# Input weights by column chunk, convolution and pool ahead of attention, residual reloads on GpSimd's DMA queue and V spills on ScalarE's

## The chip, the cores and the metric

The kernel runs on the 8 cores of one Trainium2 chip. Each core takes one prompt of 2048 tokens and 4 of the 32 decode sequences (8 tokens each), so nothing is exchanged between cores. The metric is device time in microseconds (us) of the slowest core, median of several runs.

## The reference

Two layers, each on 2080 tokens (32 sampled ones first, then the prompt) of width 1024:

```
h = rmsnorm(x, norm1_g);  u, q, k, v, gb, gc, gh = split(h @ w_in)      # 1024 x 2560
y_pool = pool_mix(u)                  # causal means over 2, 4, 8, 16 tokens, then 64x64 matrices
q, k   = rope(rmsnorm(q)), rope(rmsnorm(k))
y_attn = 3 groups of 2 heads: banded attention at window/dilation 128/1, 512/4, 2048/16,
         merged by their softmax denominators (sampled tokens attend to a cache)
y_conv = gb * conv3(gc * gh)          # causal, width 3
x = x + concat(y_pool, y_attn, y_conv) @ w_out                          # 768 x 1024
x = x + square(relu(rmsnorm(x, norm2_g) @ w_up)) @ w_down               # 1024 x 4096 x 1024
```

New pool, convolution and key/value states are also written out. Matmuls take bf16; the residual stream stays f32.

## The kernel before

Tokens are split into 5 blocks of 416 (`NB`, `BL`); a matmul has 128 rows of contraction, 128 output channels and 416 tokens. Attention goes in 4 prompt blocks of 512 tokens (`blk`) and one item for the sampled tokens (`None`).

**Who sets the order.** The order of instructions on every engine is made on the host by a planner (`Planner`, L298). Work is written as generators with a priority (the smaller number goes first) that wait for events; at each modelled moment the planner emits the ready operation with the best priority and adds its modelled cost. On the chip every engine then runs its own list strictly in order, and waits on semaphores only for real dependences (`Sched._deps`, L100), so an instruction that waits holds all that stand behind it on its engine. An event that the planner waited for is not itself a wait on the chip.

**A layer.** `norm` (L853) squares a block on ScalarE, sums on TensorE or GpSimd, and writes the normalised block `HT` by eight VectorE instructions (L889). `qkv` (L1039) makes one item of 256 tokens for one group: 16 matmuls (L1071), square, reduce, scale (L1104), GpSimd multiply (L1110), rotation (L1117, L1118), GpSimd cast (L1148), transposes. There are 24 prompt items and 3 sample items per layer, run in the order of `QORDER`. For groups 1 and 2, V goes out to DRAM and back to be reordered (`vshuffle` L1199: spill at L1200, load at L1210, both on SP's DMA queue). `att_pair`, `att_dil` and `att` do scores (L1248, L1289), exponential, and PV (L1273, L1299). `conv_item` (L988) and `pool_item` (L936) project one block with `proj` (L921, L923: 8 matmuls each) and run chains on VectorE, ScalarE and GpSimd; each block waits for the one before it. `out_proj` (L1391) adds to the residual, then `norm` again, then `up` (L1417) and `down` (L1436) in 4 chunks of the 4096 hidden channels.

**Priorities** in layer base: sample items 95, `qkv` 100 + 50 blk, `att` 90 + 50 blk, `pool_item` 120 + 40 b, `conv_item` 121 + 40 b and up.

**Memory.** The five f32 blocks of x occupy slots `SC, SP_, SQ_, SK, SV`. During attention these are scratch: convolution lives in `SC`, pool in `SP_`, qkv in `SQ_`, caches and packed queries in `SK`, V in `SV`. So x is parked in DRAM (`park` L903), and `reload` (L911) brings each block back when its slot's tenants are done, on SP's queue, before `out_proj`. One arena at `AR` holds `WQ` (q, k, v columns), `WA` (the others), the keys, `WO` and two of three `PB`, and later the MLP's `WU[0], WD[0], WU[1], WD[1]`, 16384 bytes each in this order. So the first `w_up` chunk lies over `WQ`, the first `w_down` chunk over `WQ` and `WA`.

**Loads.** `w_in` arrives in row chunks (`load_wq` L811, `load_wa` L824, two rows of 128 each, all columns), and `conv_item` and `pool_item` wait for all four `wa` chunks. The second DMA of each `wa` chunk (L827) waits for the first (L826). At the start x comes on SP's queue (`load_x0` L798; block 1 waits for a weight chunk, block 4 for the first norm; x0 and x4 share an area, x2 and x3 land in `SC` and `SP_`), weights on GpSimd's. `copy_caches` (L1458) copies old cache rows from DRAM to DRAM on SP's queue. GpSimd's queue alone casts f32 weights to bf16 on the way.

Of the kernel before, what the change touches and what calls it, by code (L numbers as in the profile page):

```python
# [24 lines left out]
NB = 5  # L25
# [272 lines left out]
class Planner:  # L298
# [3 lines left out]
    def __init__(self, S):  # L302
        self.S = S
        self.evs = {}
        self.now = 0.0
        self.seq = 0
        self.heap = []
        self.free = {e: 0.0 for e in COMPUTE + ("sp",)}
        self.ready = {e: [] for e in COMPUTE + ("sp",)}
        self.busy = {e: 0.0 for e in COMPUTE + ("sp",)}  # L310
        self.dma_free = 0.0
        self.live = 0
# [75 lines left out]
    def start(self, eng):  # L388
# [23 lines left out]
        if len(op) > 4:  # L412
            self.dma_free = max(self.dma_free, self.now) + op[4] / 230e3
            done = max(self.dma_free, self.now) + 2.0
# [71 lines left out]
def build_program():  # L486
# [103 lines left out]
    QS = M([128, 3, 64], BF16)  # L590
    KTS = M([128, 3, 32], BF16)
    for g in range(3):
        S.region(("qs", g))
        S.region(("kts", g))
# [3 lines left out]
    SS4 = [M([128, 8], F32, ("ss4", i)) for i in range(4)]  # L598
    RS4 = [M([128, 8], F32, ("rs4", i)) for i in range(4)]
    NP = 3  # L600
    PB = [M([128, 1024], BF16, ("pb", 2))]
# [21 lines left out]
    mf = Mem(MIX_OFF, M.off)  # L623
    RL = [mf([128, BL], F32, ("rl", i)) for i in range(2)]
    AT = []
    for i in range(2):
        o = mf.off
        AT.append(mf([128, 8, BL], BF16))
        for f in range(8):
            S.region(("at", i, f), o + f * 2 * BL, o + (f + 1) * 2 * BL)  # L630
    AR = M.off
    M.off += 65536
    ma = Mem(AR)
    o = ma.off
    WQ = ma([128, 8, 1152], BF16)
    for i in range(4):
        S.region(("wq", i), o + i * 4608, o + i * 4608 + 4608)
    o = ma.off
    WA = ma([128, 8, 1408], BF16)
    for i in range(4):  # L640
        S.region(("wa", i), o + i * 5632, o + i * 5632 + 5632)
# [10 lines left out]
    assert ma.off == AR + 49152  # L652
    WO = [ma([128, 2, 1024], BF16, ("wo", i)) for i in range(3)]
    PB = [ma([128, 1024], BF16, ("pb", i)) for i in range(2)] + PB
    assert ma.off == AR + 65536
    ma = Mem(AR)
    WU, WD = [], []
    for i in range(2):
        for nm, lst in (("wu", WU), ("wd", WD)):
            o = ma.off  # L660
            lst.append(ma([128, 8, 1024], BF16))
            for h in range(2):
                S.region((nm, i, h), o + h * 8192, o + h * 8192 + 8192)
# [9 lines left out]
    SLOT0 = ["m", "a", SC, SP_, "m"]  # L673
    XM = view(MIX_OFF, [128, 1, 8, BL], F32)
    XA = view(AR + 49152, [128, 1, 8, BL], F32)
    for c in range(8):
        S.region(("x", "m", c), MIX_OFF + c * BL * 4, MIX_OFF + (c + 1) * BL * 4)
        S.region(("x", "a", c), AR + 49152 + c * BL * 4, AR + 49152 + (c + 1) * BL * 4)
# [4 lines left out]
    SLOTR = [SC, SP_, SQ_, SK, SV]  # L683
# [37 lines left out]
    CVT = [m([128, 13, 128], BF16, ("cvt", 0))]  # L721
    QP = []
# [18 lines left out]
    def pool(n, fn, r, w, two=True):  # L741
        return ("pool", 0.15 + n * (0.0021 if two else 0.0011), lambda: [S.op("pool", fn, r, w)], [(0.0, r, w)])
# [18 lines left out]
    PGC, PCA, PRL, PPS, PCK, PSS, PNORM = Pool(range(2)), Pool(range(2)), Pool(range(2)), Pool(range(2)), Pool([0]), Pool(range(3)), Pool([0])  # L761

    PVST = Pool(range(3))
    evs = K.evs
# [27 lines left out]
    def prologue():  # L792
        yield ops(dve(1, lambda e: e.memset(EPSC, EPS), [], ["epsc"]),
                  pool(128, lambda e: e.memset(ONESR[:, :].bitcast(F32), 1.0), [], ["onesr"], False),
                  pool(128, lambda e: e.memset(ONESB, 1.0), [], ["onesb"], False),
                  pool(192, lambda e: e.memset(QS, 0.0), [], [("qs", g) for g in range(3)], False))

    def load_x0():  # L798
        for b in range(NB):
            Xs, s, si = stage0(b)  # L800
            if b == 1:
                yield wait(ev("wq", 0, 1))
            if b == 4:
                yield wait(ev("ht", 0, 0))
            for h in range(2):
                yield ops(ld(lambda e, h=h: e.dma_start(out=Xs[:, si, 4 * h:4 * h + 4, :], in_=xin[b, :, 4 * h:4 * h + 4, :]), 851968,
                             r=[("wq", 1)] if b == 1 else [], w=[("x", s, c) for c in range(4 * h, 4 * h + 4)], slot=("xl", s, h)))
                for c in range(4 * h, 4 * h + 4):
                    K.fire(ev("xr", 0, b, c))

    def load_wq(l, i):  # L811
        wv = w_in[l].rearrange("(c p) n -> p c n", p=128)
        yield ops(ldc(lambda e: e.dma_start(out=WQ[:, 2 * i:2 * i + 2, :], in_=wv[:, 2 * i:2 * i + 2, 256:1408]), 1179648, w=[("wq", i)], slot=("wq", i)))
# [10 lines left out]
    def load_wa(l, i):  # L824
        wv = w_in[l].rearrange("(c p) n -> p c n", p=128)
        yield ops(ldc(lambda e: e.dma_start(out=WA[:, 2 * i:2 * i + 2, 0:256], in_=wv[:, 2 * i:2 * i + 2, 0:256]), 262144, w=[("wa", i)], slot=("wa", i)),  # L826
                  ldc(lambda e: e.dma_start(out=WA[:, 2 * i:2 * i + 2, 256:1408], in_=wv[:, 2 * i:2 * i + 2, 1408:2560]), 1179648, w=[("wa", i)], slot=("wa", i)))  # L827
        K.fire(ev("wa", l, i))
# [6 lines left out]
    def load_f(l, fb, nm):  # L835
        i = fb % 2
        for h in range(2):
            if nm == "wu":
                src = w_up[l].rearrange("(c p) f -> p c f", p=128)[:, 4 * h:4 * h + 4, fb * 1024:(fb + 1) * 1024]
                dst = WU[i][:, 4 * h:4 * h + 4, :]  # L840
            else:
                src = w_down[l][fb * 1024:(fb + 1) * 1024, :].rearrange("(c p) n -> p c n", p=128)[:, 4 * h:4 * h + 4, :]
                dst = WD[i][:, 4 * h:4 * h + 4, :]
            yield ops(ldc(lambda e: e.dma_start(out=dst, in_=src), 2097152, w=[(nm, i, h)], slot=(nm, i, h)))  # L844
        K.fire(ev(nm, l, fb))
# [7 lines left out]
    def norm(l, which, b, X, s, si, src, out_ev, before=(), on_pe=False):  # L853
# [35 lines left out]
        yield ops(*[dve(BL + 100, lambda e, c=c: e.scalar_tensor_tensor(out=HT[:, c, BL * b:BL * b + BL], in0=X[:, si, c, :], scalar=NG[:, l, which, c:c + 1], in1=rst, op0=ALU.mult, op1=ALU.mult),  # L889
# [21 lines left out]
    def reload(l, b, after):  # L911
# [3 lines left out]
        for h in range(2):  # L915
            yield ops(ld(lambda e: e.dma_start(out=X[:, s, 4 * h:4 * h + 4, :], in_=src[b, :, 4 * h:4 * h + 4, :]), 851968,
                         r=([("park", b)] if l else []), w=[("x", s, c) for c in range(4 * h, 4 * h + 4)], slot=("xl", s, h)))
            for c in range(4 * h, 4 * h + 4):
                K.fire(ev("xres", l, b, c))

    def proj(l, col0, b):  # L921
        bi = yield acq(BANKS)
        yield ops(pe([(BL, lambda e, d=d: e.matmul(bank(bi)[:, 0:BL], lhsT=WA[:, d, col0:col0 + 128], rhs=HT[:, d, BL * b:BL * b + BL], start=(d == 0), stop=(d == 7)),  # L923
                       [("wa", d // 2), ("ht", b, d)], [("ps", bi)]) for d in range(8)]))
# [5 lines left out]
    def mix_free(l, b):  # L930
        if l == 0:
            return [ev("ht", 0, 0), ev("ht", 0, 4)]
        o = ORDER[l - 1][3]
        return [ev("up", l - 1, 3, x, fc) for x in o for fc in range(8)] + [ev("down", l - 1, 3, x) for x in (o[:-1] if b < 2 else o)]

    def pool_item(l, b, pc):  # L936
        yield wait(ev("ht", l, b), ev("free", l, SP_), ev("pw", l), *[ev("wa", l, i) for i in range(4)])
# [6 lines left out]
        bi = yield from proj(l, 128 * pc, b)  # L944
# [18 lines left out]
        yield ops(*[dve(L, lambda e, ps_=ps_, win=win: e.scalar_tensor_tensor(out=dt[ps_, o:BL], in0=win[ps_, 15:W], scalar=INVW[ps_, pc:pc + 1], in1=Uv[ps_, 15:W], op0=ALU.mult, op1=ALU.subtract),  # L963
# [24 lines left out]
    def conv_item(l, b, cc):  # L988
        yield wait(ev("ht", l, b), ev("free", l, SC), *[ev("wa", l, i) for i in range(4)])
# [6 lines left out]
        bc = yield from proj(l, 256 + 384 + 128 * cc, b)  # L996
# [11 lines left out]
        bh = yield from proj(l, 256 + 768 + 128 * cc, b)  # L1008
# [15 lines left out]
        for k in (1, 2):  # L1024
            o4 = [dve(L, lambda e: e.scalar_tensor_tensor(out=ca[:, o:BL], in0=Zv[:, k:k + L], scalar=cw(k), in1=ca[:, o:BL], op0=ALU.mult, op1=ALU.add), [kz, kc, "convw"], [kc])]
# [5 lines left out]
        bb = yield from proj(l, 256 + 128 * cc, b)  # L1031
# [7 lines left out]
    def qkv(l, blk, g, pr):  # L1039
# [6 lines left out]
        yield wait(ev("gqk", l), ev("vones", l), ev("qpz", l), *[ev("free", l, s) for s in (SQ_, SK, SV)], *[ev("wq", l, i) for i in range(4)], *[ev("ht", l, b) for b in hb])  # L1046
        if l > 0:
            yield wait(*[ev("um", l - 1, 3, b, fc) for b in range(NB) for fc in range(8)])
# [16 lines left out]
        def lhs(d, j):  # L1065
            if smp:
# [3 lines left out]
        wg = WQ.rearrange("p d (k n) -> p d k n", k=3)  # L1070
        yield ops(pe([(384, lambda e, d=d, j=j, jj=jj: e.matmul(pq[0:R, jj, 0:384].rearrange("p (k n) -> p k n", k=3), lhsT=lhs(d, j), rhs=wg[:, d, :, 128 * g:128 * g + 128], start=(d == 0), stop=(d == 7)),  # L1071
                       [("wq", d // 2)] + [("ht", b, d) for b in hb], [kp[jj]]) for jj, j in enumerate(tis) for d in range(8)]))
# [585 lines left out]
```

## Time and profile before

| | us |
|---|---|
| median of 3 runs (1600.55 to 1610.0) | 1606.35 |
| profiled execution, its own time | 1609.34 |
| its span on the slowest core (core 7; the others from 1582.2) | 1607.4 |
| TensorE busy in the span (89%) | 1424.3 |
| VectorE busy (53%) | 857.4 |
| ScalarE busy (30%) | 478.5 |
| GpSimd busy (22%) | 347.4 |
| DMA moved | 133.32 MB, mean 83 GB/s |

The table of stretches says for each part of the span how long each engine was busy, the TensorE clock that was granted (1.00 is the 2.4 GHz level) and the mean busy share of the 16 DMA engines. The chain of waits lists, in order of time, the pieces that ended last. An engine's timeline gives start, duration, line, operation, and in brackets the idle time before and what ended it.

### The profile page before, as it was taken

To read this page: it belongs to the slowest core of one execution; us is meant where nothing else is said; L and a number is where in the kernel's file an instruction comes from. 1 tells how busy PE (TensorE), PEld (TensorE's weight loads), DVE (VectorE), ACT (ScalarE), POOL (GpSimd) and SP (SyncE) were. 2 spreads that over 40 slices of the span, in tenths; PEclk is the share of its full clock that TensorE was granted. 3 is DMA by queue.
4 is the path that set the end of the run, shared out by engine and by line. 5 is a ranking of instruction groups with operands and counts; after the bars stand their busy time and mean duration, and the time that the engine had idled before them with its cause. 6 is when DMAs were issued, how large, how long until landed. Compare 5 with 4: busy or idle time off the path is not lost.

```text
span 1607.4 us, 26919 instructions; the slowest of 8 cores (1582.2 to 1607.4 us)
## 1 busy us (share of the span) xinstructions
PE 1424.3 (89%) x8606; PEld 801.8 (50%) x8606; DVE 857.4 (53%) x1547; ACT 478.5 (30%) x1065; POOL 347.4 (22%) x426
## 2 busy tenths in 40 slices
PE   2778788779999999999977789868699999999998
PEld 1344455434555555555544455534355555555554
DVE  1667667467444444445676666746854444444443
ACT  2544345424112212113433444532412111211211
POOL 2344344344000000012434344323500000000000
PEclk9789889899999999999999999989899999999999
DMA  8758541999223023033264452189920601400112
GB/s 184 167 75 71 111 111 34 137 234 171 49 49 58 1 53 53 1 63 76 86 148 57 68 133 74 36 127 241 169 50 1 105 1 28 79 1 1 44 69 102
DMA packets 67897, 133.32 MB, mean 83 GB/s; under 512 B 25832, under 2 KB 35112, under 8 KB 67376
## 3 DMA queue, kind: packets, MB, share of 16 engines
q0 software_dynamic: 27648, 54.14, 23.2%
q1 hardware_dynamic: 40112, 77.47, 18.1%
q8 instruction: 72, 1.18, 0.3%
q14 instruction: 65, 0.53, 0.2%
HBM read 159.71 MB, written 47.89 MB: 129 GB/s over the span
## 4 chain that ended last, share of the span: by engine, by line
PE 69%; DMA 10%; DVE 8%; issue 5%; POOL 4%; ACT 3%; SPq 1%; DVEq 0%; ACTq 0%; POOLq 0%
PE psum L1441 28%; PE psum L1425 27%; PE psum L923 5%; PE psum L1071 4%; DMA vspill<-big 4%; DMA big<-xin 3%; PE psum L1402 3%; DVE big L889 3%; DMA big<-w_in 2%; POOL sqr L875 1%; POOL big L1110 1%; POOL big L956 1%; DVE big L1118 1%; DVE big L1117 1%; DMA kv_p<-big 1%
## 5 line engine op out<-in xcount | busy, mean ns | idle before, releaser
L1425 PE MATMUL psum<-big 128*128 128x416 bf16 x2560 | 464.3, 341 | 4.3 <-DVE big L1406 2.2
L1441 PE MATMUL psum<-big 128*128 128x416 bf16 x2560 | 461.0, 339 | 1.5 <-DVE big L1431 1.5
L1430 ACT ACTIVATE big<-psum 128x416 f32<-128x416 f32 x320 | 165.1, 517 | 650.8 <-PE psum L1425 426.4
L1425 PEld LDWEIGHTS psum<-big 128*128 128x128 bf16 x2560 | 251.0, 98 | 206.8 <-issue 9.6
L1441 PEld LDWEIGHTS psum<-big 128*128 128x128 bf16 x2560 | 250.0, 98 | 201.5 <-issue 3.0
L1431 DVE TENSOR_TENSOR big<-psum,big 128x416 bf16<-128x416 f32 x320 | 187.9, 591 | 284.5 <-ACT big L1430 274.0
L1444 DVE TENSOR_TENSOR big<-psum,big 128x416 f32<-128x416 f32 x320 | 188.5, 591 | 200.4 <-PE psum L1441 199.7
L923 PE MATMUL psum<-big 128*128 128x416 bf16 x880 | 179.3, 355 | 10.6 <-ACT big L984 5.6
L1071 PE MATMUL psum<-big 128*128 128x384 bf16 (+1 forms) x816 | 156.5, 350 | 10.0 <-ACT big L1260 3.0
L889 DVE SCALAR_TENSOR_TENSOR big<-big 128x416 bf16<-128x416 f32 x160 | 120.7, 823 | 49.7 <-ACT big L886 42.6
L875 POOL TENSOR_TENSOR sqr<-sqr,big 128x416 fp32r<-128x416 f32 x98 | 107.9, 1101 | 172.1 <-ACT big L874 161.9
L923 PEld LDWEIGHTS psum<-big 128*128 128x128 bf16 x880 | 87.3, 102 | 80.5 <-issue 25.3
L1071 PEld LDWEIGHTS psum<-big 128*128 128x128 bf16 (+1 forms) x816 | 82.5, 104 | 73.9 <-issue 31.4
L1402 PE MATMUL psum<-big 128*128 128x416 bf16 x480 | 94.4, 356 | 15.4 <-DVE big L1406 13.2
L1110 POOL TENSOR_TENSOR big<-big 128x512 f32<-128x512 f32 (+1 forms) x54 | 66.7, 1238 | 184.2 <-DVE big L1104 170.2
L844 POOL DMA_DIRECT2D big<-w_up x16 | 12.2, 767 | 334.3 <-PE psum L1425 333.8
L874 ACT ACTIVATE big<-big 128x416 f32<-128x416 f32 x98 | 52.7, 547 | 98.4 <-DVE big L1406 62.5
L1402 PEld LDWEIGHTS psum<-big 128*128 128x128 bf16 x480 | 47.9, 102 | 58.3 <-issue 25.6
L956 POOL TENSOR_TENSOR big<-big 128x430 f32<-128x430 f32 (+7 forms) x72 | 64.7, 903 | 36.3 <-ACT big L952 28.4
L1406 DVE TENSOR_TENSOR big<-psum,big 128x416 f32<-128x416 f32 x80 | 45.3, 587 | 45.5 <-PE psum L1402 25.5
L864 PE MATMUL psum<-sqr,onesr 128*128 128x416 f32 x48 | 24.5, 567 | 40.3 <-ACT sqr L863 37.8
L1117 DVE TENSOR_TENSOR big<-big 128x128 f32<-128x128 f32 (+1 forms) x108 | 42.4, 393 | 27.7 <-POOL big L1110 21.8
(98 smaller groups left out, 892.9 us busy)
## 6 DMA issues: line engine op xcount, KB each, us to landing
big<-xin SPq DMA_DIRECT2D x20, 832.0 KB, 12.1
big<-w_up POOLq DMA_DIRECT2D x16, 1024.0 KB, 15.4
big<-w_down POOLq DMA_DIRECT2D x16, 1024.0 KB, 13.3
kv_s<-c SPq DMA_DIRECT2D x8, 2040.0 KB, 40.2
big<-w_in POOLq DMA_DIRECT2D x16, 576.0 KB, 8.7
xpark<-big SPq DMA_DIRECT2D x10, 832.0 KB, 3.6
big<-xpark SPq DMA_DIRECT2D x10, 832.0 KB, 15.7
yout<-big SPq DMA_DIRECT2D x20, 416.0 KB, 2.4
```

The source lines that it names most:

```text
L875: K.spawn(freeing(pool(BL, lambda e, i=i: e.tensor_tensor(out=acc, in0=acc.bitcast(F32), in1=SS[i], op=ALU.add), [ka, ("ss", i)], [ka]), P ...
L889: yield ops(*[dve(BL + 100, lambda e, c=c: e.scalar_tensor_tensor(out=HT[:, c, BL * b:BL * b + BL], in0=X[:, si, c, :], scalar=NG[:, l, wh ...
L923: yield ops(pe([(BL, lambda e, d=d: e.matmul(bank(bi)[:, 0:BL], lhsT=WA[:, d, col0:col0 + 128], rhs=HT[:, d, BL * b:BL * b + BL], start=(d ...
L956: return pool(n, lambda e: e.tensor_tensor(out=out, in0=a, in1=b_, op=ALU.add), r, w)
L1071: yield ops(pe([(384, lambda e, d=d, j=j, jj=jj: e.matmul(pq[0:R, jj, 0:384].rearrange("p (k n) -> p k n", k=3), lhsT=lhs(d, j), rhs=wg[:, ...
L1110: yield ops(pool(256 * J, lambda e: e.tensor_tensor(out=qf[0:R, 0:J, 0:256], in0=qf[0:R, 0:J, 0:256], in1=GQK[0:R].unsqueeze(1).to_broadca ...
L1402: yield ops(pe([(BL, lambda e, c=c: e.matmul(bank(bi)[:, 0:BL], lhsT=WO[c // 2][:, c % 2, 128 * oc:128 * oc + 128], rhs=mix(c, b), start=( ...
L1425: yield ops(pe([(BL, lambda e, d=d: e.matmul(bank(bi)[:, 0:BL], lhsT=WU[i][:, d, 128 * fc:128 * fc + 128], rhs=HT[:, d, BL * b:BL * b + BL ...
L1430: yield ops(act(BL, lambda e: e.activation(out=RL[ri], in_=bank(bi)[:, 0:BL], func=AF.Relu), [("ps", bi)], [("rl", ri)]))
L1431: yield ops(dve(BL, lambda e: e.tensor_tensor(out=AT[a][:, fc, :], in0=bank(bi)[:, 0:BL], in1=RL[ri], op=ALU.mult), [("ps", bi), ("rl", ri ...
L1441: yield ops(pe([(BL, lambda e, f=f: e.matmul(bank(bi)[:, 0:BL], lhsT=WD[i][:, f, 128 * oc:128 * oc + 128], rhs=AT[a][:, f, :], start=(f == ...
L1444: yield ops(dve(BL, lambda e: e.tensor_tensor(out=X[:, s, oc, :], in0=bank(bi)[:, 0:BL], in1=X[:, s, oc, :], op=ALU.add), [("ps", bi), ("x ...
```

## The change

- `w_in` is loaded by columns: `WQ` as three chunks (q, k, v), `WA` as four tiles c, h, p, b; `proj` waits for its own tile only.
- At the start all of x and `w_in` is issued on GpSimd's queue in one order: x0, x1, c, h, b, p, x2, x3, q, k, v, x4. Blocks 2, 3 and 4 land in `SQ_, SK, SV`, so `SC` and `SP_` are free at once and qkv waits for the norms of blocks 2, 3 and 4.
- `pool_item` and `conv_item` get priorities 90 + 15 b and 91 + 15 b and up.
- Reloads go on GpSimd's queue, one process per half; blocks 0 and 1 swap slots. V spills go on ScalarE's queue.
- The arena's order is `WD[0], WU[0], WU[1], WD[1]` with `WU[0]` over c, h and p. The first `w_up` chunk waits for convolution and pool, the first `w_down` chunk for qkv, the second `w_up` chunk for `out_proj` too.
- `RL` moves beside `AT`; `up` waits for `out_proj` of two blocks instead of three or four. `QS` and `SS4` move into slot `SK`.
- The planner's costs change for some VectorE and GpSimd operations, and it models side queues.
- The next layer's c, h, p come after its last use of `WU[0]`, q, k, v after the third `w_down` chunk, b after the last `w_up` chunk.

```diff
-    SLOT0 = ["m", "a", SC, SP_, "m"]
+    SLOT0 = ["m", "a", SQ_, SK, SV]
-    SLOTR = [SC, SP_, SQ_, SK, SV]
+    SLOTR = [SP_, SC, SQ_, SK, SV]
...
+    for nm, lst, i, off in (("wd", WD, 0, 0), ("wu", WU, 0, 18432), ("wu", WU, 1, 34816), ("wd", WD, 1, 51200)):
...
+    def lda(fn, nbytes, r=(), w=(), slot=None):
+        return ("act", 0.45, lambda: [S.dma(fn, reads=r, writes=w, slot=slot, queue="act")], [(0.0, r, w)], nbytes)
...
+    def load_x(b, h):
+        Xs, s, si = stage0(b)
+        yield ops(ldc(lambda e: e.dma_start(out=Xs[:, si, 4 * h:4 * h + 4, :], in_=xin[b, :, 4 * h:4 * h + 4, :]), 851968,
+                      w=[("x", s, c) for c in range(4 * h, 4 * h + 4)], slot=("xl", s, h)))
...
+        c0, n = WCOL[nm], 256 if nm == "p" else 384
+        yield ops(ldc(lambda e: e.dma_start(out=WA[nm], in_=wv[:, :, c0:c0 + n]), 4096 * n, w=[("wa", nm)], slot=("wa", nm)))
...
-            yield ops(ld(lambda e: e.dma_start(out=X[:, s, 4 * h:4 * h + 4, :], in_=src[b, :, 4 * h:4 * h + 4, :]), 851968,
...
+        yield ops(ldc(lambda e: e.dma_start(out=X[:, s, 4 * h:4 * h + 4, :], in_=src[b, :, 4 * h:4 * h + 4, :]), 851968,
...
-    def proj(l, col0, b):
+    def proj(l, nm, i, b):
+        yield wait(ev("wa", l, nm))
...
-        yield ops(ld(lambda e: e.dma_start(out=vspill[g - 1, blk, pr].rearrange("(j p) c -> p j c", p=128), in_=VST[vi]), 98304, r=[("vst", vi)], w=[("vd", g, pr)], slot=("vsp", g, pr)))
+        yield ops(lda(lambda e: e.dma_start(out=vspill[g - 1, blk, pr].rearrange("(j p) c -> p j c", p=128), in_=VST[vi]), 98304, r=[("vst", vi)], w=[("vd", g, pr)], slot=("vsp", g, pr)))
...
-            yield wait(*[ev("om", l, x, oc) for x in range(3 + k) for oc in range(8)])
+            yield wait(*[ev("om", l, x, oc) for x in (2 * k, 2 * k + 1) for oc in range(8)])
...
-            for s in (SQ_, SK, SV):
+            for s in (SC, SP_):
                 K.fire(ev("free", 0, s))
...
-                K.spawn(pool_item(l, b, pc), base + 120 + 40 * b)
+                K.spawn(pool_item(l, b, pc), base + 90 + 15 * b)
             for cc in range(3):
-                K.spawn(conv_item(l, b, cc), base + 121 + 40 * b + cc)
+                K.spawn(conv_item(l, b, cc), base + 91 + 15 * b + cc)
...
-                wu, wd = qk_done, qk_done + proj_done
+                wu, wd = proj_done, qk_done
             elif fb == 1:
-                wu, wd = att_done + proj_done, out_done + att_done
+                wu, wd = att_done + proj_done + out_done, out_done + att_done
...
+    x_loads = lambda b: [load_x(b, h) for h in range(2)]
+    K.spawn(loads([], 1, *x_loads(0), *x_loads(1), load_wa(0, "c"), load_wa(0, "h"), load_wa(0, "b"), load_wa(0, "p"), load_pw(0),
+                  *x_loads(2), *x_loads(3), *[load_wq(0, i) for i in range(3)], *x_loads(4)), 1)
+    K.spawn(loads([ev("ht", 0, 1)], 3, *[load_wo(0, i) for i in range(3)]), 3)
```

## Rows read from the trace of the kernel before

**Rows 1.** Busy time by stretch; columns: stretch, length, engines (instructions), granted clock, DMA share, GB/s.
```profile
0.00:21.00 21.00, 2.25 (x4) 1.14 (x4) 0.06 (x1) 3.26 (x5) 8.45 (x20) 1.00 0.88 174
21.00:90.00 69.00, 42.52 (x153) 21.48 (x153) 38.01 (x76) 33.37 (x93) 15.57 (x20) 0.84 0.66 157
90.00:298.00 208.00, 176.24 (x1300) 104.87 (x1300) 141.87 (x289) 93.04 (x223) 87.46 (x118) 0.91 0.54 86
298.00:379.00 81.00, 56.16 (x323) 30.52 (x320) 46.41 (x73) 23.43 (x45) 32.00 (x32) 0.87 1.01 194
379.00:831.00 452.00, 450.43 (x2561) 250.46 (x2559) 219.47 (x368) 109.67 (x214) 58.39 (x62) 1.00 0.29 60
831.00:847.00 16.00, 5.82 (x30) 2.83 (x29) 10.00 (x26) 6.04 (x25) 4.38 (x10) 0.78 0.83 159
847.00:1060.00 213.00, 181.13 (x1354) 108.08 (x1351) 145.66 (x302) 98.09 (x245) 91.81 (x118) 0.95 0.38 74
1060.00:1175.00 115.00, 83.16 (x468) 45.17 (x468) 76.29 (x109) 36.68 (x72) 43.42 (x41) 0.87 1.01 195
```

**Rows 2.** TensorE's timeline: start, us, line, tile, count [idle before, what ended it].
```profile
50.16 5.12 PE L1071 MATMUL psum<-big 128*128 128x384 bf16 x16
...
167.99 1.01 PE L1248 MATMUL psum<-big 128*128 128x256 bf16 x4 [8.51 <-DVE big L1104]
...
318.23 1.93 PE L1299 MATMUL psum<-big 128*128 128x32 bf16 x32
...
855.14 2.76 PE L1071 MATMUL psum<-big 128*128 128x384 bf16 x16
...
901.80 2.76 PE L1071 MATMUL psum<-big 128*128 128x384 bf16 x16
...
1082.77 1.87 PE L1299 MATMUL psum<-big 128*128 128x32 bf16 x32 [13.19 <-DMA big<-vspill]
```

**Rows 3.** The chain of waits in order of time: start, us, what.
```profile
6.48 17.01 DMA big<-w_in
...
123.92 16.31 DMA vspill<-big
142.22 23.61 DMA vspill<-big
...
1055.06 18.48 DMA vspill<-big
```

**Rows 4.** TensorE's groups of instructions in 21 to 90 us.
```profile
L1071 PE MATMUL psum<-big 128*128 128x384 bf16 (+1 forms) x104 | 25.0, 414 | 0.0
L864 PE MATMUL psum<-sqr,onesr 128*128 128x416 f32 x32 | 17.0, 584 | 30.2 <-ACT sqr L863 27.7 <-ACT big L1101 1.8 <-ACT big L1161 0.2
```

**Rows 5.** TensorE's projection group in 832 to 1148 us.
```profile
L923 PE MATMUL psum<-big 128*128 128x416 bf16 x440 | 88.2, 352 | 6.2 <-ACT big L984 5.6 <-ACT big L1293 0.6
```

**Rows 6.** VectorE's groups in 832 to 1148 us, shapes kept apart.
```profile
L889 DVE SCALAR_TENSOR_TENSOR big<-big 128x416 bf16<-128x416 f32 x32 | 29.7, 997 | 2.6 <-ACT big L886 1.5 <-ACT big L1101 1.1
...
L1025 DVE SCALAR_TENSOR_TENSOR big<-big 128x416 f32<-128x416 f32 x24 | 17.3, 722 | 3.2 <-ACT big L1017 2.6
...
L963 DVE SCALAR_TENSOR_TENSOR big<-big 64x416 bf16<-64x416 f32 x16 | 13.3, 831 | 1.0 <-DVE big L963 0.5
...
L1032 DVE TENSOR_TENSOR big<-psum,big 128x416 bf16<-128x416 f32 x15 | 8.8, 587 | 7.4 <-PE psum L923 7.0 <-PE psum L1154 0.3
L1009 DVE TENSOR_TENSOR big<-psum,big 128x416 f32<-128x416 f32 x12 | 7.0, 587 | 1.4 <-PE psum L923 1.2
```

**Rows 7.** SP's timeline of DMA issues around the long spills.
```profile
124.35 0.80 SPq L1462 DMA_DIRECT2D kv_s<-c  x1
...
141.51 0.61 SPq L1462 DMA_DIRECT2D kv_s<-c  x1
```

**Rows 8.** DMA issues by kind: count, KB each, median us from issue to landing.
```profile
big<-xpark SPq DMA_DIRECT2D x10, 832.0 KB, 15.7
...
vspill<-big SPq DMA_DIRECT2D x32, 96.0 KB, 2.8
```

More of the change, by code:

```diff
@@ L311, in __init__ @@
         self.dma_free = 0.0
+        self.side = {e: 0.0 for e in ("sp", "act")}
         self.live = 0
@@ L412, in start @@
         if len(op) > 4:
-            self.dma_free = max(self.dma_free, self.now) + op[4] / 230e3
-            done = max(self.dma_free, self.now) + 2.0
+            t = op[4] / 230e3
+            if eng == "pool":
+                self.dma_free = max(self.dma_free, self.now) + t
+                done = self.dma_free + 2.0
+            else:
+                self.side[eng] = max(self.side[eng], self.now) + (2 * t if self.dma_free > self.now else t)
+                self.dma_free += t
+                done = self.side[eng] + 2.0
             made[-1].fin = done
@@ L721, in build_program @@
     CVT = [m([128, 13, 128], BF16, ("cvt", 0))]
+    o = m.off
+    QS = m([128, 3, 64], BF16)
+    for g in range(3):
+        S.region(("qs", g), o + 128 * g, o + 128 * g + 128)
+    SS4 = [m([128, 8], F32, ("ss4", i)) for i in range(4)]
     QP = []
@@ L833, in load_wo, with load_f, loads @@
         K.fire(ev("wo", l, i))
-    def load_f(l, fb, nm):
+    def load_f(l, fb, nm, h):
         i = fb % 2
[L837 to L845, printed above, removed]
+        if nm == "wu":
+            src = w_up[l].rearrange("(c p) f -> p c f", p=128)[:, 4 * h:4 * h + 4, fb * 1024:(fb + 1) * 1024]
+            dst = WU[i][:, 4 * h:4 * h + 4, :]
+        else:
+            src = w_down[l][fb * 1024:(fb + 1) * 1024, :].rearrange("(c p) n -> p c n", p=128)[:, 4 * h:4 * h + 4, :]
+            dst = WD[i][:, 4 * h:4 * h + 4, :]
+        yield ops(ldc(lambda e: e.dma_start(out=dst, in_=src), 2097152, w=[(nm, i, h)], slot=(nm, i, h)))
+        K.fire(ev(nm, l, fb, h))
+    def loads(waits, prio, *gens):
+        if waits:
+            yield wait(*waits)
+        for i, g in enumerate(gens):
+            K.spawn(g, prio + 0.01 * i)
     def seq(waits, *gens):
@@ L909, in park, with reload @@
         K.fire(ev("parked", l, b))
-    def reload(l, b, after):
+    def reload(l, b, h, after):
         yield wait(*after)
@@ L988, in conv_item @@
     def conv_item(l, b, cc):
-        yield wait(ev("ht", l, b), ev("free", l, SC), *[ev("wa", l, i) for i in range(4)])
+        yield wait(ev("ht", l, b), ev("free", l, SC))
         if b > 0:
@@ L1151, in qkv @@
             yield wait(*[ev("S", l, blk - 1, g, p) for p in ((0, 1) if g == 1 else (pr,) if g == 0 else (0,))])
+        if l > 0 and not smp:
+            yield wait(*[ev("um", l - 1, 3, b, fc) for b in range(NB) for fc in range(8)])
         bt = yield acq(BANKS)
@@ L1438, in down @@
         a, s = k % 2, SLOTR[b]
[L1439 removed]
+        yield wait(ev("wd", l, fb, 0), ev("wd", l, fb, 1), *[ev("up", l, fb, b, fc) for fc in range(8)])
         bi = yield acq(BANKS)
@@ L1510, in mixer @@
         for b in range(NB):
-            K.spawn(reload(l, b, done[SLOTR[b]]), base + 300 + b)
+            for h in range(2):
+                K.spawn(reload(l, b, h, done[SLOTR[b]]), base + 300 + b + 0.5 * h)
             K.spawn(out_proj(l, b), base + 410 + b)
```

164 lines of the change are left out of this document (64 added, 100 removed).

## The prediction

> **What bounds the kernel now.** I read the table of stretches first [rows 1]. In the MLP (379 to 831 us, and again to the end) TensorE is busy 450.43 of 452 us at full clock: nothing in this change can gain there. All idle time of TensorE lies in the mixers and around them. Before 21 us it does 2.25 us of work; from 21 to 90 us it is busy 42.52 of 69; in the body of attention 176.24 of 208 and 181.13 of 213 (0.85 in both); in the passage from attention to the MLP 56.16 of 81 in layer 0 and 83.16 of 115 in layer 1; at the border of the layers 5.82 of 16. The DMA share in the same table tells the passages from the rest: 1.01 in both, so 16 engines without a gap, against 0.54 and 0.38 in the bodies. The start has 0.66 although everything waits for loads there: transfers are issued late, not slowly.
>
> The chain of waits says the same in pieces [rows 3]: a `w_in` chunk for 17.01 us at the start, then V spills that take 16.31, 23.61 and 18.48 us, where the median spill lands in 2.8 us [rows 8]. TensorE's timeline gives what those cost it: 8.51 us idle ahead of 167.99 and 13.19 us ahead of the last PV of layer 1 [rows 2]. So there are three bounds, one after the other: issue of the first loads, then TensorE with the latency of attention's chain, then DMA in the passage.
>
> **The start.** Today 21 to 90 us holds 25.0 us of qkv matmuls and 17.0 us of norm sums [rows 4]. The change takes qkv out of this stretch, since it needs the norms of blocks 2, 3 and 4 now, and puts convolution and pool in. What fits? VectorE: a norm is eight instructions of 997 ns, 8.0 us a block; the four largest groups of convolution and pool sum to 17.3 + 13.3 + 8.8 + 7.0 = 46.4 us for five blocks, 9.3 each [rows 6]. At 17.3 us a block 69 us hold 4.0 blocks. TensorE: projections are 88.2 us for five blocks, 17.6 each [rows 5]; at the body's 0.85 it does 58.6 us of work in 69 us, less 17.0 of norm sums leaves 41.6, or 2.4 blocks. TensorE is the tighter: 41.6 in place of 25.0, 16.6 us of work brought forward, worth 16.6 / 0.85 = 20 us later. The data are there: by 90 us the DMA engines have done 0.88 x 21 + 0.66 x 69 = 64 us of work, and x0, x1 and the four tiles are 9.2 of the 19.0 MB of x and `w_in`; issued without waits on GpSimd's queue they are in by some 37 us, the first tile by some 22. **Take -20.** Ends: 0, if the tiles come no sooner; -32, if TensorE has no gap from 21 to 90 (69 - 17.0 - 25.0 = 27, over 0.85). The memsets and the GpSimd adds of pool stand behind the issues on GpSimd, which is busy 15.57 of 69 us; constants stay on SP's queue.
>
> **The V spills.** Moved to ScalarE's queue, a spill no longer stands behind cache copies in SP's. But of the three long spills only the one at 142.22 had a copy issued just ahead of it, at 141.51; the copy at 124.35 came after the spill at 123.92 [rows 3, 7], which took 16.31 us all the same. Contention is mostly in the engines that all queues share. I take half of the 8.51 us: **-4**, ends 0 and -8.5. The Trainium skill, *DMA: Bandwidth & Descriptors*, section *Issuing engines are not separate DMA queues*, speaks against any gain: transfers of all issuing engines run on the same 16 DMA engines, and spreading them saves issue time only. By that rule this term is 0 and the sum 4 us less; the spill at 123.92 agrees with it, the one at 142.22 leaves it open. The load back (L1210) stays on SP behind the copies. ScalarE takes the 32 issues in its own order, each behind the copy that filled the buffer; it is busy 93.04 of 208 us, so they cost nothing unless the DRAM region's last load is late, and then ScalarE's squares and exponentials stand behind it.
>
> **The border.** 10.2 us idle in 831 to 847 [rows 1]. The c, h and p tiles are loaded during the last MLP chunk instead of at its end, so pool (block 0) can go at once; convolution still needs the last block's norm and park, as its slot holds that block. I take half, **-5**, ends 0 and -10.
>
> **The passages.** Idle 81 - 56.16 = 24.8 us and 115 - 83.16 = 31.8 us, together 56.6 [rows 1]. What leaves them: reloads of blocks 0 and 1 (3.4 MB) and the first `w_up` chunk (2.1 MB as written), 5.5 MB a layer, which at 194 GB/s is 28 us a layer, 56 in all. So the idle time and the transfers that leave are of one size. `out_proj` of blocks 0 and 1 and the first `up` can run inside attention, in the place of the convolutions that went ahead, and the last V load, behind 18.48 us of spill today, meets less traffic. Against it: blocks 2, 3 and 4 and the first `w_down` chunk now stand in one queue, and their slots come free no sooner. I take three quarters, **-42**. Ends: -13, only the wait ahead of the last PV goes; -75, all idle time and the 0.13 of clock missing from 139 us of busy time (18 us) go too. What is late next is the reload of block 3, after the last `att`.
>
> **Costed at nothing.** The traffic that leaves goes into the bodies, whose DMA share is 0.54 and 0.38: hidden there, unless it meets a spill; with that cover gone 13.19 us a layer. The 20 reload issues on GpSimd stand among qkv's multiplies and casts; GpSimd is busy 87.46 of 208 us, so the issues hide, but a reload that waits for its slot holds the next multiply and with it a whole qkv item. The chunks' shorter runs move as many bytes. Attention that loses convolution as its filler gets `out_proj` and `up` in exchange: 0, upper end in the second rival. The wait of the second `w_up` chunk for `out_proj` has a whole MLP chunk (a quarter of 452 us) to hide in. New planner costs alter order only.
>
> **The sum:** -20 - 4 - 5 - 42 = -71 from the profiled execution's 1609.3, so 1538. The median of the runs is 3 us below that execution, so 1535.
>
> **Rivals.**
> - *The passage stays bound by transfers.* `w_down` and the reloads share a queue, and cache copies on SP follow at once. For it: share 1.01 [rows 1]. Against: 28 us a layer less to move. Then only the 13 us go: -42, 1564 against the median.
> - *Reloads get slower on GpSimd's queue*, so that the passages keep their length: -29, 1577. Against it: both passages run at share 1.01 with weights issued by GpSimd while VectorE is busy 46.41 of 81 and 76.29 of 115 us. The Trainium skill, *SBUF — State Buffer*, section *Who interferes with whom*, has such a rule: a DMA issued from GpSimd starves while VectorE holds the port that they share. No row here shows it.
> - *Attention keeps its own pace (slower).* From the first prompt item to the last PV are 268 us in layer 0 and 228 in layer 1 [rows 2]. If that is the pace of attention's chain, and convolution was free beside it, then a later first item is paid in full. It moves from 50 to 90 us or more in layer 0 (+40), and in layer 1 behind projections of two blocks with better priority (2 x 17.6 = +35). With -42 - 4 - 5 from the rest that is +24: 1630. It decides at the pace: 228 us for 24 items are 9.5 us each. Against it: from 855.14 to 901.80 eight items start in 47 us, 5.8 each, and TensorE is 0.85 busy in both bodies, so it is not waiting for one chain.
> - *The change doesn't do what it says.* Blocks of convolution and pool wait for one another; if they end as late as now, the early `w_up` chunk isn't early, the slots come free no sooner, and the start gains on one side what qkv loses on the other. Only the border's 5 us stay: 1601.
>
> **How the numbers follow.** My forecast has a chance of 0.55, the first rival 0.15, the second 0.05, the slower one 0.15, the last 0.10. About 0.5% (8 us) can be told from no change here, so below 1598 is faster and above 1614 slower. Faster: 0.55 + 0.15 + 0.05 and a little of the last, 0.77; same 0.09; slower 0.14. With all terms at their weak ends the sum is -13, with all at their strong ends -125: 1593 to 1481 against the median. For 8 in 10 I take 1485 to 1600: it holds the first two rivals and nearly all of my case, and leaves out the slower rival and some of the last.
>
> **What would show it.** In the profile after: projection matmuls from some 25 us on, and TensorE busy 55 us or more in 21 to 90; the first prompt qkv item near 90; the first `w_up` issue before the last qkv item; `out_proj` of blocks 0 and 1 ahead of the last PV; the passages with under 15 us idle each; spills still over 10 us where reloads run. The forecast is wrong if attention from first item to last PV stays above 230 us in layer 0, if TensorE's share in the bodies falls below 0.8, or if the passages keep a DMA share of 1.0 for 80 us or more.

## The result, and the profile after

The changed kernel takes 1670.19 us against 1606.35: ratio 1.0389, 95% interval 1.0309 to 1.0468, so it is slower by some 62 us where the forecast was 71 faster. (A median of so few runs can hold a disturbed one; ratios are made without those, and below the ratio counts.)

The table of stretches, cut for the changed kernel at the same places of its work as [rows 1], as near as its order allows:

```profile
0.00:21.00 21.00, 5.63 (x10) 2.87 (x10) 0.90 (x3) 7.70 (x14) 12.90 (x26) 1.00 0.88 210
21.00:105.00 84.00, 30.78 (x122) 14.67 (x121) 18.41 (x40) 11.48 (x25) 3.89 (x10) 0.72 1.05 136
105.00:365.00 260.00, 210.51 (x1437) 122.73 (x1437) 176.94 (x350) 116.65 (x290) 111.33 (x140) 0.90 0.40 78
365.00:445.00 80.00, 42.52 (x261) 25.18 (x259) 25.34 (x45) 18.55 (x40) 18.48 (x22) 0.74 0.82 172
445.00:890.00 445.00, 439.56 (x2480) 243.46 (x2478) 221.11 (x362) 108.00 (x212) 62.45 (x64) 0.99 0.30 57
890.00:935.00 45.00, 32.02 (x172) 16.62 (x171) 26.30 (x64) 14.56 (x44) 15.70 (x28) 0.96 0.39 71
935.00:1147.00 212.00, 184.55 (x1368) 111.74 (x1367) 159.58 (x306) 101.36 (x246) 99.05 (x119) 0.95 0.45 99
1147.00:1235.00 88.00, 56.93 (x353) 31.69 (x350) 47.43 (x68) 24.39 (x46) 27.44 (x30) 0.84 0.70 153
```

Three places of layer 0 lost time. From 21 to 105 us TensorE is idle for 53.2 of 84 us while the DMA share is 1.05: nothing is issued late any more, and yet the data that matter are not there. In the body of layer 0 it is idle for 49.5 of 260 us, against 31.8 of 208, and in the passage behind it for 80 - 42.52 = 37.5 us, against 24.8 [rows 1]. The passage of layer 1 only failed to gain: 88 - 56.93 = 31.1 us idle, against 31.8. Layer 1's body (0.87 busy) and the MLP stand about as before. The chain of waits names the transfers (start, us, what; answers to [rows 3]):

```profile
4.79 32.56 DMA big<-w_in
...
42.06 30.89 DMA big<-sconv
...
73.95 29.09 DMA big<-spool
...
240.70 24.63 DMA vspill<-big
...
372.42 11.14 DMA vspill<-big
...
393.83 34.26 DMA big<-xin
```

`sconv` is a load of 4 KB and `spool` one of 30 KB: the last rows of convolution and pool that the sampled requests carry over. In the same time GpSimd's queue moved 3.56 and 3.87 MB. SP's timeline shows why there are two in a row:

```profile
9.26 5.91 SPq L1009 DMA_DIRECT2D big<-sconv  x2
41.41 0.61 SPq L1027 DMA_DIRECT2D conv_s<-big  x1
42.06 0.97 SPq L1009 DMA_DIRECT2D big<-sconv  x1
43.13 30.77 SPq L1027 DMA_DIRECT2D conv_s<-big  x2
73.95 2.44 SPq L954 DMA_DIRECT2D big<-spool  x2
...
385.56 3.85 SPq L1469 DMA_DIRECT2D kv_s<-c  x6
```

A store of new rows (`conv_s`, L1027) waits for the result that it stores, the next load stands behind it on SP, and the next store waits for that load (30.77 us). The last row answers to the copies of the kernel before, which were issued behind eight reloads in SP's own queue; now the reloads are on GpSimd's queue and the copies run beside them. SP's timeline of the kernel before:

```profile
315.58 11.48 SPq L916 DMA_DIRECT2D big<-xin  x8
327.11 3.65 SPq L1462 DMA_DIRECT2D kv_s<-c  x6
```

What each queue moved in two stretches (queue, packets, MB, share of the 16 engines; q0 is GpSimd's, q1 SP's): first 42.06 to 72.95, then 393.83 to 428.1 us:

```profile
q0 software_dynamic: 2006, 3.56, 93.7%
q1 hardware_dynamic: 1489, 0.01, 5.9%
...
q1 hardware_dynamic: 167, 4.56, 72.5%
q0 software_dynamic: 250, 1.54, 20.5%
```

In the first, SP's queue gets 1489 packets through in 30.89 us, 48 a microsecond in the mean, for 0.01 MB. (Some 1024 of them are the load and the store ahead of it; the others belong to the store issued behind it at 43.13.) In the second it is the other way round: the copies' packets are of 27 KB, and they hold 72.5% of the engines' time, so the reloads crawl. The landing times by kind (count, KB each, median us) answer to [rows 8]: the reloads have doubled from 15.7, the spills are little changed from 2.8:

```profile
big<-xpark POOLq DMA_DIRECT2D x10, 832.0 KB, 30.8
...
vspill<-big ACTq DMA_DIRECT2D x32, 96.0 KB, 3.6
...
big<-spool SPq DMA_DIRECT2D x4, 30.0 KB, 21.5
big<-sconv SPq DMA_DIRECT2D x6, 4.0 KB, 12.4
```

The bytes of the start also cost the engines more than before. In its first 90 us the kernel before moved 14.46 MB in 64 us of the 16 engines' time (71.2% of 90); in its first 105 us the changed one moved 15.85 MB in 107 us (101.8%). The queues' rows of these two stretches, the kernel before first:

```profile
q0 software_dynamic: 3136, 4.72, 36.8%
q1 hardware_dynamic: 4048, 9.69, 34.4%
...
q0 software_dynamic: 9544, 15.15, 93.8%
q1 hardware_dynamic: 5878, 0.67, 8.0%
```

### The profile page after: what moved, and what is told of

Its sections match the earlier page's. It is cut to its first block, busy times and chain, and to the rows that moved or that the text cites. A ratio compares the mean times of both kernels' runs of the same rounds, so it can differ in the third digit from the quotient of the medians.

```text
span 1668.0 us, 27005 instructions; the slowest of 8 cores (1635.9 to 1668.0 us)
## 1 busy us (share of the span) xinstructions
PE 1429.3 (86%) x8606; PEld 805.9 (48%) x8606; DVE 861.2 (52%) x1547; ACT 482.2 (29%) x1065; POOL 359.3 (22%) x447
## 4 chain that ended last, share of the span: by engine, by line
PE 66%; DMA 15%; DVE 9%; issue 5%; POOL 2%; ACT 2%; DVEq 0%; ACTq 0%; SPq 0%; POOLq 0%
PE psum L1431 26%; PE psum L1448 26%; PE psum L1075 5%; PE psum L930 4%; PE psum L1408 3%; DMA vspill<-big 3%; DMA big<-spool 3%; DMA big<-sconv 2%; DMA big<-xin 2%; DMA big<-w_in 2%; DVE big L896 2%; DMA big<-xpark 2%; DVE big L1121 1%; POOL big L1114 1%; DVE big L1098 1%
## 5 line engine op out<-in xcount | busy, mean ns | idle before, releaser
L1431 PE MATMUL psum<-big 128*128 128x416 bf16 x2560 | 465.9, 341 | 10.2 <-DVE big L1412 7.3
L1412 DVE TENSOR_TENSOR big<-psum,big 128x416 f32<-128x416 f32 x80 | 45.3, 586 | 67.4 <-DMA big<-xin 24.8
L1121 DVE TENSOR_TENSOR big<-big 128x128 f32<-128x128 f32 (+1 forms) x108 | 48.7, 451 | 31.4 <-POOL big L1114 22.5
```

What stands on the lines that cost most here:

```text
L1121: yield ops(*[dve(122 * J, lambda e, k=k: e.tensor_tensor(out=rot[k], in0=xr, in1=tb[k], op=ALU.mult), [kq, "rope"], [kr]) for k in range(2)])
```

## The experiments

The planner's order shifts everywhere when one cost moves, so the edits are made behind it: `by` finds transfers in the planned list by their kind (`zs` loads of `sconv`, `us` of `spool`, `c2c` cache copies, `xl` x and its reloads, `wo` `w_out`, `vsp` V spills, `so_cs` stores to `conv_s`, `kvo` the sampled rows' stores to `kv_s`), `move` puts them elsewhere in it, and every wait is then worked out anew from what is read and written. All engines keep their order but the queue named; r7, r10 and r12 also add small copies on ScalarE and GpSimd. The diffs give the edits in short.

| run | kernel and edit | ratio to before | 95% |
|---|---|---|---|
| | after | 1.0389 | 1.0309 to 1.0468 |
| r1 | histories first | 1.0217 | 1.0174 to 1.0259 |
| r2 | histories together | 1.0191 | 1.0149 to 1.0232 |
| r3 | six copies late | 1.0104 | 1.0075 to 1.0132 |
| r4 | reloads on SP | 1.0081 | 1.0046 to 1.0116 |
| r5 | spills on SP | 1.0345 | 1.0295 to 1.0395 |
| r6 | r2 and r3 | 0.9851 | 0.9797 to 0.9904 |
| r7 | histories staged | 1.0161 | 1.0137 to 1.0184 |
| r8 | before, six copies late | 0.9988 | 0.9972 to 1.0005 |
| r9 | r2, all twelve copies late | 0.9794 | 0.9768 to 0.9819 |
| r10 | r9, staged, `w_out` behind | 0.9706 | 0.9682 to 0.9730 |
| r11 | before, all copies late | 0.9977 | 0.9946 to 1.0008 |
| r12 | r10, `w_out` further behind | 0.9788 | 0.9755 to 0.9822 |

**The histories moved (r1, r2).**

```diff
+    move(by("zs")[:3] + by("us")[:2], 0)                      # r1: first on SP's queue
+    move(by("zs")[2:3] + by("us")[:2], by("zs")[1:2])         # r2: behind the first two
```

> Kernel after, every engine's order kept, but layer 0's five history loads (three of sconv, two of spool) are issued first on SyncE's queue. Theory H (the five small loads of many descriptors, late and one behind the other beside GpSimd's full queue, hold up conv and pool): TensorE idles for some 47 us between 40 and 105 us in the kernel after; most of that goes, so 1670 falls by 35 to 55 us, to 1615 to 1635, and the histories land before 25 us. Rival C (the start is held up by the column chunks of w_in, which carry runs of 768 bytes): the start stays as it is, 1660 to 1675. Rival P (the plan of the mixer has grown longer, wherever its start lies): under 15 us.

> Kernel after, every engine's order kept, but the third sconv load and the two spool loads are issued right behind the first two sconv loads (about 9 us) instead of behind the conv_s stores. Theory H says that each small descriptor waits for its turn beside the GpSimd queue, so the five share one pace: the first two landed 22 us after issue, 1024 of them, which is 47 a microsecond; 2560 are through at about 63 us, where the last landed at 103 us before. So 20 to 40 us less, 1630 to 1650, between the kernel after and the run with the loads first. If what costs is a fixed latency of some 30 us a load, all five are in by 42 us and the gain equals that of the loads first (35 to 55 us). Rival C: no change.

Measured: 0.0172 and 0.0198 under after, 28 and 32 us at 1606. Rival C as the whole cause falls: the column chunks are the same in both, and the start got shorter. What the chunks themselves cost is not tested by it. Both are over the 15 us of rival P. r1 stays under the 35 to 55 us that theory H gave it; the histories then delay `norm_g`, the gain of the first norm, on SP's queue (16.75 us on r1's chain, from 19.40), and the first projection starts at 37.05 us, in after at 26.66. r2 is inside its range. By its total it didn't tell pace from a fixed latency, as it gave as much as r1. Its last history was issued at 20.65 us and landed 34.9 us later, at 55.6: nearer to the 63 of one pace than to the 42 of a fixed latency.

**The histories staged (r7).**

```diff
-    e.dma_start(out=ZS[:, cc, :, 0:2], in_=sconv[l, cc])      # 512 pieces of 8 bytes; spool likewise, of 60
+    e.dma_start(out=ZST[cc], in_=sconv[l, cc].rearrange("p n r -> p (n r)"))   # 128 pieces of 32
+    e.copy(out=ZS[:, cc, :, 0:2], in_=n4(ZST[cc]))            # ahead of the first reader, on its engine
```

> Kernel after, the history loads at their own places, but each into a contiguous tile (128 descriptors of 32 or 240 bytes rather than 512 of 8 or 60), from which ScalarE or GpSimd copies the columns on. Theory H by descriptors (each waits for its turn beside the GpSimd queue): a load lands in 5 to 10 us instead of 22 to 31, and the start gives back as much as with the loads moved, in both layers: 1615 to 1640. If what costs is a latency of each load, whatever its descriptors, landing stays at 20 to 30 us and the time within 10 us of 1670.

Measured: 0.0228 under after, 37 us. But the two loads on the chain took 24.08 and 18.82 us, not 5 to 10 (first the chain, then the queues from 36.75 to 60.83 and from 61.76 to 80.58 us):

```profile
36.75 24.08 DMA big<-sconv
...
61.76 18.82 DMA big<-spool
```

```profile
q1 hardware_dynamic: 1164, 0.01, 5.4%
...
q1 hardware_dynamic: 826, 0.06, 9.1%
```

A load stands in SP's queue behind the store issued just ahead of it, whose 512 pieces of 8 bytes were left as they were (in r7 the store issued at 36.04 landed at 58.77 us and the load behind it at 60.83); I had forgotten those. Landing follows the packets in the queue only in part: load and store ahead fell from 1024 to 640 packets and the landing from 30.89 to 24.08 us; the two `spool` loads with their store fell from 1536 to 768, the landing of the first of them from 29.09 to 18.82. The mean pace over a landing, 44 to 50 packets a microsecond (1164 in 24.08 us, 826 in 18.82, 1489 in 30.89, 1468 in 29.09), is not one steady pace either. In after, from 20 to 25 us and then from 41.41 to 50 us:

```profile
q0 software_dynamic: 832, 0.63, 98.2%
q1 hardware_dynamic: 831, 0.03, 23.1%
...
q0 software_dynamic: 527, 1.77, 103.9%
q1 hardware_dynamic: 88, 0.00, 1.0%
```

In the first SP's queue sends 166 packets a microsecond, one for each of GpSimd's. In the second, just behind the issue of store and load, it sends 10 a microsecond. Why so few is open. The Trainium skill, *DMA: Bandwidth & Descriptors*, section *Queues, rings and completion order*, has each DMA engine take turns between the rings that have work, a packet at a time; the first stretch agrees, with 831 packets for 832, and the second does not show it. r7 doesn't exclude a fixed part of the landing, then. What it shows is the price: fewer pieces gave 37 us. Some 17 us of it are the two landings. Another 6 come from a tile of `w_in`: in after TensorE waits for it until 37.49 us and has its first 40 projection matmuls done at 41.98, in r7, without that wait, at 35.70.

**The copies held, the reloads moved back (r3, r4), and the same copies in the kernel before (r8).**

```diff
+    for o in by("c2c")[6:12] + by("c2c")[18:24]:              # r3, r8: the six issued at each passage
+        o.rw[0].append(("ht", 4, 7))                          # wait for block 4's second norm
+    for o in by("xl")[10:]:                                   # r4: the 20 reloads
+        o.eng, o.dma_slot = "sp", ("xr",) + o.dma_slot[1:]
```

> Kernel after, same orders, but SyncE holds the six cache copies of either layer that it issues at the passage until block 4's second norm is done. Theory Q (the reloads on GpSimd's queue share the 16 engines with copies that stood behind them in SyncE's own queue before): reloads land in 16 to 22 us instead of 30, and each of the two passages is 8 to 14 us shorter: 1643 to 1655. Theory L (the reloads come late by their waits, and the copies cost nothing): 1665 to 1672.

> Kernel after, the 20 reloads issued on SyncE's queue again, at the same places of the order. Theory Q: the copies stand behind the reloads again and the reloads land in 16 to 22 us; but SyncE now holds what follows (V loads, key and value stores) behind the reload's wait, and the queue shares with w_down: 1645 to 1668. If GpSimd's queue itself is slower or quicker for these transfers than SyncE's, the reloads of blocks 0 and 1, which meet no copies, change their time to land by over 20%.

> Kernel before, all orders kept, the same six copies of either layer held until block 4's second norm. Theory Q: in the kernel before they stood behind the reloads in SyncE's own queue, so holding them gains little: 1597 to 1610 (the tail of the reloads shares engines with them only once the first have gone). If copies beside a passage cost as much in the kernel before, it falls by 30 us or more, to 1560 to 1577, and the queue move is not what made them matter.

Measured: r3 0.0285 and r4 0.0308 under after, 46 and 49 us, where theory Q gave at most 27 and 25, so both times lie under its ranges. Both put the copies behind the reloads, one by a wait, one by the queue, and agree within their intervals; r8 gave 0.0012, so in the kernel before these copies cost next to nothing. In r3 the queues from 392.4 to 409 us, and the two passages in the table of stretches:

```profile
q0 software_dynamic: 748, 4.47, 82.0%
```

```profile
365.00:445.00 80.00, 62.65 (x373) 36.28 (x371) 48.36 (x76) 25.93 (x53) 33.23 (x37) 0.85 0.55 128
...
1124.00:1190.00 66.00, 56.35 (x358) 31.84 (x356) 49.12 (x70) 25.85 (x49) 28.45 (x31) 0.96 0.51 128
```

GpSimd's queue now moves 4.47 MB in 16.6 us where it moved 1.54 in 34.3. The passages are idle for 17.4 and 9.7 us, against 37.5 and 31.1 in after. GpSimd's queue is not slow in itself: the median reload of layer 1 took 11.4 us on it in r3 and 10.0 on SP's in r4, and the eight reloads of blocks 0 and 1, where r4's expectation looked for 20%, took 9.9 us in the mean in after and 9.6 in r4.

**The spills (r5).** `for o in by("vsp"): o.eng = "sp"`.

> Kernel after, the 32 V spills issued by SyncE again at the same places of the order. If the move to ScalarE's queue saved what its term said (4 us, between 0 and 8.5), this is 0 to 9 us slower than after: 1670 to 1679. Rival: issues on ScalarE cost its in-order compute time (32 of 0.4 to 0.6 us, and waits with work behind them), and then this is faster: 1650 to 1665.

Measured: ratio 1.0345, its interval over that of after. No difference is shown, in either direction; the intervals are some 16 us wide, so the 4 us of the term are neither shown nor excluded.

**Both mendings (r6).** The edits of r2 and r3 together.

> Kernel after with both mendings: the five history loads issued together early, and the six copies of either layer held to the end of the passage. Alone they gave 30 us (1670 to 1640) and 47 us (1670 to 1623). If they lie at different places of the time, they add: 1590 to 1600, faster than the kernel before (1607). If the start's gain is swallowed later (attention waits for the same weights and the copies), 1605 to 1620.

Measured: 0.0538 under after, 86 us, where the two alone sum to 0.0483: within the intervals they add. The kernel is now faster than the one before. Its chain in layer 0's attention still holds

```profile
162.06 21.01 DMA vspill<-big
...
208.25 24.72 DMA vspill<-big
```

**All copies out of attention (r9, r11), and the border (r10, r12).**

```diff
+    for n in (0, 12):                                         # r9, r10, r11, r12
+        move(by("c2c")[n:n + 6], L.index(by("c2c")[n + 6]))
+        for o in by("c2c")[n:n + 12]:
+            o.rw[0].append(("ht", 4, 7))
+    move(by("wo")[3:6], [by("so_cs")[5]])                     # r10: layer 1, behind the last conv_s store
+    move(by("wo")[n:n + 3], [by("kvo")[11 * (n + 1)]])        # r12: n = 0, 3; behind the sampled kv_s stores
```

> The kernel with both mendings (1590), but with all twelve cache copies of a layer held to the end of its passage, the six that ran inside attention too. Theory V (what is left of the missing gain is lost in attention: the V spills, 256 small descriptors each, wait 21 and 25 us in layer 0 beside copies, reloads and w_up): the wait beside copies (25 us at 208 to 233) shrinks to 5 to 12 us, that beside the reload (21 us at 162 to 183) stays; 10 to 20 us less in layer 0 and 0 to 8 in layer 1: 1562 to 1580. If the Pool queue's loads alone make the spills wait: 1584 to 1592. If twelve copies crowd the MLP's loads: over 1592.

> Kernel before, all orders kept, with all twelve copies of a layer held to block 4's second norm. It tells what of the gain by later copies belongs to the change: if the copies inside attention hindered the kernel before as well, it falls by 8 to 25 us, to 1582 to 1600; if its longer attention had room for them: 1602 to 1610.

> As the run before (all copies late, history loads together), and in addition the history loads go to contiguous tiles (a quarter of the descriptors), and layer 1's three w_out loads are issued behind the last history load of that layer. Theory H: layer 1's border holds spool 15.2 and sconv 11.9 us on the chain beside w_out; these shrink to 3 to 6 us, and the start gives 0 to 10 us more: 10 to 25 us under the run before, 1540 to 1570. If the border waits for something else behind the history loads: within 6 us of the run before.

> As the run before it (1561), but the three w_out loads of either layer are issued behind the twelve small stores of the sampled rows' keys and values (8 KB each, 256 elements a descriptor), which in layer 1 stood beside them: 14.3 us on the chain at 849 us. Theory H, for a third kind of small transfer: that store lands in 2 to 5 us, and the run is 4 to 14 us quicker, 1547 to 1557; in layer 0 the full stretch of the engines ends some 12 us sooner and costs or gives 0 to 4 us. Rival: what delays the next projection there is the chain of norms and pools itself, and the time stays within 3 us of 1561.

Measured: r9 takes 1573.98, inside theory V's range, and is 0.0057 (9 us) under r6 by ratio, with intervals that overlap. The same edit gives the kernel before 0.0023, with 1 in its interval. r9's chain in that stretch:

```profile
161.42 13.69 DMA vspill<-big
```

The wait at 208 us, which had copies beside it (half of the engines' time, 49.6%), is gone from the chain. The one at 161 us stays, if shorter, and theory V's reload is not what it waits beside: r9's first reload is issued at 190.39 us, while two loads of cached keys and values on GpSimd's queue (issued at 159.74 and 160.34) run then. r10 is 0.0088 (14 us) under r9, at 1561.44, and is the quickest version that was run: 0.9706. From 21 to 90 us TensorE is busy 54.31 of 69 us in it, and the passages are idle for 12.8 + 2.9 us (layer 0, in two pieces) and 5.9 us (layer 1):

```profile
21.00:90.00 69.00, 54.31 (x249) 27.41 (x248) 44.17 (x89) 26.67 (x59) 19.67 (x37) 0.95 1.10 148
...
303.00:350.00 47.00, 34.20 (x219) 21.25 (x217) 20.72 (x41) 14.69 (x31) 13.00 (x17) 0.80 0.72 179
350.00:383.00 33.00, 30.14 (x160) 15.89 (x158) 26.52 (x33) 11.22 (x23) 20.35 (x20) 0.95 0.33 45
...
1050.00:1104.00 54.00, 48.07 (x321) 28.15 (x320) 37.33 (x61) 22.87 (x46) 24.21 (x27) 0.97 0.56 152
```

Which of r10's two edits gave the 14 us was not tried. r12 missed, on the slow side of both its ranges: the wait at which it aimed in r10's chain of layer 1,

```profile
848.77 14.31 DMA kv_s<-big
```

is not in its own chain, and its profiled span is shorter (1552.9 us, r10 1559.0), yet its ratio is 0.0082 over r10's (1566.87). So the wait can go without a gain in time; where the runs lose, I didn't find.

## Why the prediction was wrong

**The start (-20).** The work could be brought forward, nearly by the size forecast, and its price was missing. With the histories out of the way TensorE does 54.31 us of work in 21 to 90 (r10), where I had asked for 55; that is 11.8 us more than the 42.52 before, where I had counted 16.6. In after it is 30.46. The step that failed is "constants stay on SP's queue", in a paragraph that moved convolution and pool into the stretch and counted their matmuls, their VectorE groups and their GpSimd adds, but not their own transfers: five loads and five stores in 8 to 60 byte pieces. In the kernel before those of layer 0 lay in a stretch with share 0.54 and landed in under 4 us (`spool`) and 7.6 to 12.2 us (`sconv`); here they met a share of 1.05, in an order where each load stands behind a store. That is 28 to 37 us (r1, r2, r7), more than the term. I had written that the start's share of 0.66 means "issued late, not slowly"; filling it made the small transfers beside it slow.

**The V spills (-4).** Not shown: r5 finds no difference, but couldn't have seen 4 us. The Trainium skill, *DMA: Bandwidth & Descriptors*, section *Issuing engines are not separate DMA queues*, gave 0, and r5 agrees with it no less than with -4. The long spills stayed (24.63 and 11.14 us on the chain of after).

**The border (-5).** It brought no gain in after: 890 to 935 us has 13.0 us idle, against 10.2, with `spool` (13.97 us) and `sconv` (6.92 us) on the chain beside `w_out`. In r10, 810 to 836 us has 4.5.

**The passages (-42).** The mechanism came as forecast: the last PV of layer 0 ends at 393 us, `out_proj` of two blocks and the first `up` are done by then, and `down` runs at once. Then the reload took 34.26 us and gave it all back: 68.6 us idle in the two passages, against 56.6 before. The step that failed is the count of what leaves the passage. I subtracted 5.5 MB a layer and left the copies where they stood; moving the reloads off SP's queue took away the order that kept the copies behind them. My first rival named the copies, but only let the passage stay as it was, for -42 in all; nothing in it made the change slower. With the copies held, the passages lose 56.6 - 27.0 = 29.6 us against before (r3), and 56.6 - 21.6 = 35.0 in r10: 70 and 83% of what I took was there.

**Costed at nothing.** "Hidden there, unless it meets a spill" was needed: in r6 the spills that meet reloads, `w_up` and copies stand on the chain for 21.01 and 24.72 us. I had priced that at 13.19 us a layer. The part that copies make of it is small (9 us in r9, not clear of the intervals). "The chunks' shorter runs move as many bytes" was a second term put at nothing without a price: the same x and `w_in`, with `w_in` in runs of 768 bytes and `w_out` behind them, took 107 us of the engines' time where the kernel before needed 64 for 14.46 MB. In r2, with the histories out of the way, the longest piece of the start's chain is a tile of `w_in` (48.25 us). How much of this is the shorter runs, and what it costs the kernel, no run separates, as none has row chunks again. The issues on GpSimd show no cost that r4 could tell.

**The rivals.** The slower side had 0.14, but for another mechanism. From the first prompt item (168.86) to the last PV (391.20) are 222 us in after, 268 before [rows 2], so attention's length alone doesn't decide against the 228 us that the slower rival took for its pace. But a later first item was not paid in full: in r10 it starts 72 us later than before (122.41), and the last PV 12 us later (330.69). Reloads that are slower on GpSimd's queue don't show either: they land in 11.4 us there, where the copies are held. So these rows don't show what the Trainium skill, *SBUF — State Buffer*, section *Who interferes with whom*, says of transfers that GpSimd issues beside a VectorE that holds the port the two share.

**The signs.** None of the three signs of being wrong came: attention took 222 us and not over 230, the bodies were 0.81 and 0.87 busy, and the passages had shares of 0.82 and 0.70. All three watch a length or a share; none watches when a load that somebody waits for lands. Of the positive signs the work of TensorE in 21 to 90, the first prompt item and the idle time of the passages failed at once.

**What it sums to.** The forecast ratio was 1535 / 1606.35 = 0.9556. Of the 0.0833 by which after misses it, 0.0683 (110 us) came back in r10 by moving transfers alone: histories, copies, and layer 1's `w_out`. Some 24 us stay open, and the rows don't put them in one place. TensorE is idle for 133 us of r10's span against 183 before, 50 less (its busy time is the same within 2 us) where I forecast 71: 35.2 in layer 0's body (110 to 303 us) against 31.8, 26.6 in layer 1's against 31.9, and 11.9 from 1104 us on against 5.4 from 1175 on. The first prompt item starts at 122 us, not at 90, but TensorE is busy for 29.6 of the 30 us ahead of 120. Spills of 16.19 and 9.99 us are still on the chain of layer 0, beside loads of GpSimd's queue; that these loads are the cause was not tried alone.

## What to carry to other kernels

When work is moved into a stretch whose DMA engines are full, list every transfer that goes with it, by number of pieces and by what stands ahead of it, and not by bytes alone: a load of 4 KB in 512 pieces, with a store of 512 pieces ahead of it in its queue, took as long as 3.56 MB of x and weights. When a transfer changes queue, ask what the old queue had kept behind it; an order that nobody wrote down is lost with the move. Long DRAM copies are best issued where nobody waits for anything on any queue, here inside the MLP, where twelve of them cost nothing that the time shows.

## What the runs showed of the hardware

- Small packets on SP's queue went one for one with GpSimd's where both had work: 831 beside 832 packets of `w_in` from 20 to 25 us of after, 166 a microsecond, and 1611 beside 1617 from 20 to 30 us of r2. Over the landing of a load on the chain the mean was only 44 to 50 a microsecond, in four stretches of two kernels, whether they held 0.01 or 0.06 MB; at the head of one of them SP's queue sent 88 packets in 8.6 us.
- In one stretch large packets took most of the engines' time: copies in packets of 27 KB held 72.5% of it against 20.5% for loads that moved 6 KB a packet.
- The issuing queue of a 96 KB spill (ScalarE's or SP's) made no difference that these intervals, some 16 us wide, could show.
